# Moving a norm beside the other half's projection, finishing output projections tile by tile, and writing the output in four parts

## What is computed

```python
x = x + gt1 * y_lat
x = x + gt2 * squared_relu_mlp(modulate_2(rms_norm(x, norm2_g[i]), sh2, sc2), mlp_w1[i], mlp_w2[i])
if not last:
    ctx = ctx + mods_c[2] * y_ctx
    ctx = ctx + mods_c[5] * squared_relu_mlp(modulate_2(rms_norm(ctx, norm2_g[i]), mods_c[3], mods_c[4]), mlp_w1[i], mlp_w2[i])
```

## Time and profile before

| what | value |
|---|---|
| median of 3 runs | 3119.28 us |
| lowest and highest run | 3113.44 and 3119.92 us |
| profiled execution, first to last instruction (span) | 3114.3 us |
| own time of the profiled execution | not listed apart from the three runs |
| mean granted clock of TensorE | 0.967 of full |
| TensorE busy | 2933.0 us |
| VectorE, ScalarE busy | 1225.4, 714.7 us |
| moved by DMA | 687.00 MB, 221 GB/s |

### The profile page before, as it was taken

How to read it: one execution, slowest core, us unless ns; L and a number is a source line. 1 busy time by engine, 2 the same in 40 slices (tenths; PEclk the granted TensorE clock), 3 DMA queues, 4 the chain that set the end, 5 groups by cost and what they waited for, 6 DMA issues and landing times.

```text
span 3114.3 us, 51962 instructions
## 1 busy us (share of the span) xinstructions
PE 2933.0 (94%) x23528; PEld 2024.0 (65%) x23528; DVE 1225.4 (39%) x2176; ACT 714.7 (23%) x1144; POOL 47.5 (2%) x37
## 2 busy tenths in 40 slices
PE   5898998998999999999999899889999999988898
PEld 5788997877333333333333466689999885687898
DVE  5668853242111101101101277445555443454454
ACT  2224333131000000000000112334333322311343
POOL 0000000000000000000000000000000000032000
PEclk8899999999999999999999999999999999999999
DMA  7756764536899999999999322046566431010452
GB/s 288 290 201 256 286 232 170 196 120 253 327 364 358 364 368 372 356 362 376 366 354 364 135 68 95 1 149 230 217 230 227 166 123 53 1 71 6 165 182 82
DMA packets 96947, 687.00 MB, mean 221 GB/s; under 512 B 10576, under 2 KB 13776, under 8 KB 13904
## 3 DMA queue, kind: packets, MB, share of 16 engines
q1 hardware_dynamic: 94064, 678.47, 56.6%
q10 hardware_dynamic: 2656, 5.14, 0.4%
HBM read 682.52 MB, written 1.05 MB: 219 GB/s over the span
## 4 chain that ended last, share of the span: by engine, by line
PE 90%; DVE 6%; ACT 3%; DMA 1%; issue 1%; POOL 0%; DVEq 0%; ACTq 0%
PE ps L485 40%; PE ps L1942 19%; PE ps L821 11%; PE ps L1965 7%; PE ps L732 6%; PE ps L1968 3%; PE ps L496 2%; PE ps L709 1%; PE ps L1950 1%; DMA XT<-XIN 1%; DVE macc L578 1%; ACT HT L670 1%; DVE FR L802 0%; DVE RN L680 0%; DVE AR L2438 0%
## 5 line engine op out<-in xcount | busy, mean ns | idle before, releaser
L1942 PE MATMUL ps<-AR 128*32 128x512 f32 x4080 | 533.5, 592 | 0.0
L485 PE MATMUL ps<-HT,ring 128*128 128x256 f32 (+1 forms) x1696 | 446.2, 424 | 9.6 <-ACT HT L670 9.6
L485 PEld LDWEIGHTS ps<-HT,ring 128*128 128x128 f32 x1696 | 326.6, 194 | 122.4 <-issue 79.7
L485 PE MATMUL ps<-FR,FR 128*128 128x256 f32 x3120 | 389.9, 285 | 1.7 <-DVE M_moe_mod L587 1.7
L485 PEld LDWEIGHTS ps<-FR,FR 128*128 128x128 f32 x3120 | 379.5, 192 | 11.5 <-issue 9.5
L2053 DVE TENSOR_TENSOR AR<-AR,ps 128x256 f32<-128x256 f32 x84 | 35.5, 423 | 802.1 <-ACT AR L2017 802.1
L821 PE MATMUL ps<-FR,FR 128*128 128x256 f32 x2832 | 349.3, 283 | 0.0
L821 PEld LDWEIGHTS ps<-FR,FR 128*128 128x128 f32 x2832 | 343.9, 192 | 0.8 <-issue 0.8
L1942 PEld LDWEIGHTS ps<-AR 128*32 128x32 f32 x4080 | 150.8, 110 | 297.0 <-issue 294.5
L802 DVE TENSOR_TENSOR FR<-ring,FR 128x2048 fp32r<-128x2048 f32 x129 | 294.4, 2291 | 116.1 <-ACT FR L786 116.1
L786 ACT ACTIVATE FR<-ring 128x2048 fp32r<-128x2048 f32 x129 | 244.6, 1906 | 120.2 <-PE ps L821 92.6
(11 more groups left out here) (411 smaller groups left out, 2603.6 us busy)
## 6 DMA issues: line engine op xcount, KB each, us to landing
ring<-W SPq DMA_DIRECT2D x441, 1024.0 KB, 6.2
AR<-W SPq DMA_DIRECT2D x205, 1024.0 KB, 7.9
XT<-XIN ACTq DMA_DIRECT2D x2, 1024.0 KB, 16.8
cst<-CS ACTq DMA_DIRECT2D x1, 1851.0 KB, 35.7
out<-XT SPq DMA_DIRECT2D x1, 1024.0 KB, 4.5
sml<-SM ACTq DMA_DIRECT2D x1, 986.5 KB, 32.5
cst<-CS ACTq DMA_DIRECT2D x1, 129.5 KB, 7.6
C<-SM ACTq DMA_DIRECT2D x1, 4.0 KB, 5.2
```

Source lines behind the costliest of these rows:

```text
L485: ins = g.matmul(out, l, r, **kw)
L1942: ins = g.matmul(bank.ap[group(i), :], mo.hg[e % 2][:, 4 * h + k, group(t)], w[n][:, k, :], start=j == 0 and k == 0, stop=j == 1 and k == ...
```

## The change

1. `early_step` replaces the rule of the background steps in block 0's network: one step in each of the 17 rounds of half 0 and in the first six of half 1. The rest of `ada1` no longer stands in the odd mixer.
2. `down_slot` and `down3` go through their last slot tile by tile (`down_order`), both k of a tile before the next, and raise an event `two` after every second tile; `residual_dve` waits for these one after another.
3. In `even_pe` the norm's sums of m0, half 0, come after the first slot of `ev.down1`. `ev.end` is gone. VectorE does the residual of half 0, the first low half, the norm of half 0, two more low halves, and then the residual of half 1. ScalarE makes three high halves before round 0. The banks of `ev.down1` are kept until round 1. The buffers ev.C and ev.oD, which the projection reads, are put at the end of the arena, behind the network's splits.
4. In m0's second half the norm of the odd mixer's half 0 is made: squares on ScalarE after round 8, sums on TensorE after round 9, root after round 10, products and shift after round 11. The banks of `m0.down1` are kept until the second input projection.
5. The output is written in four transfers of two tiles each, each issued once the second of its tiles is done.

```diff
+def early_step(block, c, r):
+    return 1 if block == 0 and (c == 0 or r < 6) else 0
...
+        def down_order(last):
+            return [(kk, m) for m in range(8) for kk in range(2)] if last else [(kk, m) for kk in range(2) for m in range(8)]
...
-            for kk in range(2):
-                k = 2 * i + kk
-                for m in range(8):
+            for kk, m in down_order(i == n - 1):
...
+                if i == n - 1 and kk == 1 and m in (1, 3, 5):
+                    ins.then_inc(*s.done("two", x, m // 2))
...
         def residual_dve(g, s, x, ready, M, gate_at, c=0):
-            s.wait_ge(*ready)
             for m in range(8):
+                s.wait_ge(*(("two", x, m // 2) if m < 6 else ready))
...
             for i in range(4):
                 out(1, i, [("ev.og", 3)] if i == 2 else [])
-            down_end("ev.down1")
-            s.mark("ev.end")
+                if i == 0:
+                    norm_pe(g, s, "m0")
...
-            for c in range(2):
-                residual_dve(g, s, f"ev.down{c}", ("down", f"ev.down{c}", 3), MN["ada0"][0], 16, c)
-            s.mark("ev.end")
+            residual_dve(g, s, "ev.down0", ("down", "ev.down0", 3), MN["ada0"][0], 16, 0)
...
         def mlp_pe(g, s, q, bg):
-            norm_pe(g, s, p)
-            s.wait_marks(mlp_before(q)[1], "TVAG")
+            if q:
+                norm_pe(g, s, p)
+                s.wait_marks("od.end", "TVAG")
...
+                    if n == 1 and q == 0:
+                        down_end("ev.down1")
...
-                    if q == 0 and (r % 2 or r % 4 == 2):
-                        bg.go()
+                    bg.go(early_step(q, c, r))
...
+                    if n == 16 + 9:
+                        norm_pe(g, s, "odd")
...
         def mlp_act(g, s, q):
...
             shift_act(g, s, p, MN[f"ada{q}"][0], 24, mlp_pairs(q)[0])
+            if q == 0:
+                w.make_act(g, s, 3)
...
+                    if n == 16 + 8:
+                        squares_act(g, s, "odd", odd_ready(s), 0)
+                    if n == 16 + 10:
+                        norm_root_act(g, s, "odd", 0)
+                    if n == 16 + 11:
+                        shift_act(g, s, "odd", MN["ada1"][0], 0)
...
         def mlp_dve(g, s, q, bg):
...
+            if q == 0:
+                w.make_dve(g, s, 3)
+                residual_dve(g, s, "ev.down1", ("down", "ev.down1", 3), MN["ada0"][0], 16, 1)
...
-                    if q == 0 and (r % 2 or r % 4 == 2):
-                        bg.go()
+                    bg.go(early_step(q, c, r))
+                    if n == 16 + 11:
+                        norm_dve(g, s, "odd", HT, mod_weight("ada1", 0))
...
-            norm_pe(g, s, "odd", (0,))
             b = counts.take("od.f1")
             s.wait_emptied(b)
             mm(g, b.ap[0:64, 0:256], [(sm("hy_w1", p=(0, 33)), cs("zT", p=(0, 33)))]).then_inc(*s.done("od.f1_ps"))
-            bg.finish("ada1")
-            s.wait_marks("m0.end")
             norm_done(s, "odd", (0,))
             both("od.in", 0)
             norm_pe(g, s, "odd", (1,))
             both("od.in", 1)
+            down_end("m0.down1")
...
+            for k in (0, 2, 4, 6):
+                s.wait_ge("norm.x", "fin1", k + 1, 0)
+                g.dma_start(OUT.rearrange("(k p) t -> p k t", p=128)[:, k:k + 2, :], XT[:, k:k + 2, 0:256]).then_inc(s_out, 16)
             s.barrier("end")
-            g.dma_start(OUT.rearrange("(k p) t -> p k t", p=128), XT[:, :, 0:256]).then_inc(s_out, 16)
-            g.wait_ge(s_out, 16)
+            g.wait_ge(s_out, 64)
```

More of the change, by code:

```diff
@@ L725, in down_slot @@
                 s.wait_ge(*one_ready)
[L726 to L733 removed]
+            for kk, m in down_order(i == n - 1):
+                k, h = 2 * i + kk, m % 2
+                if k == 0:
+                    s.wait_emptied(acc[m // 2])
+                ins = g.matmul(acc[m // 2].ap[:, h * 256:h * 256 + 256], w[:, kk, m * 128:m * 128 + 128], rhs(k),
+                               start=k == 0 and h == 0, stop=k == 2 * n - 1 and h == 1, skip_group_check=True)
+                if i == n - 1 and kk == 1 and m in (1, 3, 5):
+                    ins.then_inc(*s.done("two", x, m // 2))
             ins.then_inc(*s.done("down", x, i, frees=(sl,) if free else ()))
@@ L811, in up3, with down3 @@
             return mm(g, out, [q for k in range(8) for q in three([x[:, k, :] for x in v], [x[:, k, :] for x in hs])])
[L813 to L823, removed]
+        def down3(g, s, x, pair, i, n, acc, hid):
+            w = [v.rearrange("p (k c) -> p k c", k=2) for v in pair]
+            for kk, m in down_order(i == n - 1):
+                h = m % 2
+                if i == 0 and kk == 0:
+                    s.wait_emptied(acc[m // 2])
+                for j, (l, r) in enumerate(three([v[:, kk, m * 128:m * 128 + 128] for v in w], [v[:, kk, :] for v in hid])):
+                    ins = g.matmul(acc[m // 2].ap[:, h * 256:h * 256 + 256], l, r,
+                                   start=i == 0 and kk == 0 and h == 0 and j == 0,
+                                   stop=i == n - 1 and kk == 1 and h == 1 and j == 2, skip_group_check=True)
+                if i == n - 1 and kk == 1 and m in (1, 3, 5):
+                    ins.then_inc(*s.done("two", x, m // 2))
             return ins
@@ L1399, in dense_pe @@
                     s.wait_ge("dn.lo", i).wait_ge("dn.d_lo", n - 1)
-                    down3(g, s, w.pair(i), n - 1, 11, acc, [x[:, (n - 1) % 3, :, :] for x in de.d]).then_inc(*s.done("dn.used", i))
+                    down3(g, s, "dn.down", w.pair(i), n - 1, 11, acc, [x[:, (n - 1) % 3, :, :] for x in de.d]).then_inc(*s.done("dn.used", i))
                 bg.go()
@@ L2522, in mlp_pe @@
                         s.wait_ge(p + ".lo", i).wait_ge(p + ".d_lo", n - 1)
-                        down3(g, s, w.pair(i), r - 1, 16, acc, [x[:, (n - 1) % 3, :, :] for x in m.d]).then_inc(*s.done(p + ".used", i))
-                    if q == 0 and (r % 2 or r % 4 == 2):
-                        bg.go()
-                    if n == 4 and T == 512:
+                        down3(g, s, f"{p}.down{c}", w.pair(i), r - 1, 16, acc, [x[:, (n - 1) % 3, :, :] for x in m.d]).then_inc(*s.done(p + ".used", i))
+                    bg.go(early_step(q, c, r))
+                    if n == 4 and q == 0:
                         norm_pe(g, s, p, (1,))
-                for k in range(4):
-                    counts.drop(f"{p}.down{c}", k)
+                    if n == 16 + 9:
+                        norm_pe(g, s, "odd")
+                if q or c == 0:
+                    down_end(f"{p}.down{c}")
             s.mark(p + ".end")
@@ L2533, in mlp_act @@
             m, p, T = ml[q], f"m{q}", 512 - 256 * q
-            ready, before = mlp_before(q)
-            norm_act(g, s, p, ready(s))
-            s.wait_marks(before, "TVAG")
+            norm_act(g, s, p, mlp_ready(s, q))
+            if q:
+                s.wait_marks("od.end", "TVAG")
             w = Splits(p, m.names, m.fr, PARTS, from_ring)
```

33 lines of the change are left out of this document (15 added, 18 removed).

## The result

| | before | after |
|---|---|---|
| median, four runs of each | 3117.38 us | 3091.45 us |
| lowest and highest run | 3113.44 and 3119.92 | 3088.98 and 3093.42 |
| span of the profiled execution | 3114.3 | 3089.8 |
| mean granted clock of TensorE | 0.967 | 0.970 |

The ratio is 0.992, interval 0.9909 to 0.9932: 25.9 us less by the medians, 24.5 by the spans. Forecast were 3093.6 us and a gain of 25.7. The gain agrees to 0.2 us and the time to 2.2: the forecast started from 3119.28, the median of three runs of the kernel before, and over four runs it is 3117.38. The profiled execution itself took 3091.74 us, 1.9 more than its span. Most lines of the file moved down: the earlier trace rows speak of L709 and L691, which are L713 and L695 now, L821 is L828, L485 is L489.

What follows compares the result with a forecast made beforehand. TensorE, busy 94%, bounds the kernel, its idle time at a few seams deciding. 11.06 + 8.8 - 0.4 + 3.9 + 2.3 = 25.7 us off the median 3119.28 gives 3093.6 us, range 3082 to 3107.

Steps and rivals of the forecast that it cites:

- Part 1: Even mixer to m0: norm of m0's latent half beside the context projection removes idle time and slow clock; gain 11.06 us.
- a seam keeps its wait: Rival: norm done early, but m0's first up-projection waits for another thing; 11.06 us back, 3104.7 us; chance 0.14.
- Part 2: m0 to odd mixer: norm of the odd mixer's latent half inside m0's second half; gain 8.8 us.
- Part 3: Background steps move forward; neutral on TensorE except a longer wait between m0's halves; loss 0.4 us.
- rival of the starved rounds: Slower rival: m0's rounds with three slots each let the weight ring fall behind; 3128.1 us at 1.5 us a round; chance 0.05.
- Part 4: Last slot tile by tile wins only idle time before norm sums at ssm, odd and m1: 1.3 us each, 3.9 together.
- whole-residual rival: Each of three norm sums at ssm, odd and m1 gets its 3.23 us; 5.8 us more gone, 3087.8 us; chance 0.06.
- Part 5: Program's end: output in four parts, the last landing 2.2 us after its issue; gain 2.3 us.
- rival of outputs in a row: Output parts go one after the other at the program's end; 2.3 becomes -2.0 us, 3097.9 us; chance 0.06.
- slow 8.59 us: m0's first up-projection group, 5.92 us one group later; two causes left undivided: waiting for low halves, and clock at 0.50.

Runs made afterwards that it cites:

- run with 7 us of cover: Changed kernel with the norm's sums of m0 moved behind the third slot of the context projection instead of the first; 3096.3 us, ratio 0.9942.
- run without cover: Changed kernel with the norm's sums of m0 moved behind the fourth and last slot of the context projection; 3106.13 us, ratio 0.9963.
- the last one: Changed kernel with m1's first split made early, eight output transfers, and two background steps moved behind the residuals they stood before; 3081.79 us, ratio 0.9888.
- plain-order: Changed kernel, run twice, with each last slot through all eight tiles for one k, then the other, residual after the last matmul; 3100.47 and 3097.77 us.
- keep-busy run: Changed kernel with 17 matmuls whose result nobody reads behind m1's norm sums, to keep TensorE busy; 3094.91 us, ratio 0.993.
- unedited kernel: The changed kernel run once more without any edit, beside later experiments; 3088.94 us, ratio 0.9909.

## Why the prediction was right

*Part 1.* The two timelines decided it: TensorE waits for low halves that VectorE had been free to make for 25 us. Cost and mechanism held, with 11.4 for 11.06 and 9.9 when undone. The condition for full gain was a chain of 13.5 us and a queue of about 18 under a cover of 20.9. From the end of the sums, 2039.20, the chain took 12.8 us, to 2052.02, and the queue with its two low halves 18.6, to 2057.77. (The prediction speaks of ten steps of VectorE in the chain; there are sixteen, a product and a low half for each of eight k, and they took 6.4 us for its 7.) The run with 7 us of cover shows the loss on the other side of that condition, and the rival "a seam keeps its wait" is what the run without cover looks like: 11.0 us lost in the trace for its 11.06. (Its median of 3106.13 is near the rival's 3104.7 by chance, as it has some us of other stages in it.)

*Part 2.* 8.8 to 9.0 for 8.8; undone, 7.7. The difference is mostly how far the clock fell behind the idle time, 9.24 us for the projection there and 10.14 in the earlier trace rows.

*Part 3.* The wait between the halves went from 0.97 to 1.33. The cost was 0.36 for 0.4, and the rounds stayed free: TensorE was busy in 203.00 of 203 us of the first half's rounds and in 100.00 of 100 us of the second's, so the rival of the starved rounds falls. No experiment undoes this part; in the last one the wait goes with the step's place, as this account says.

*Part 4.* 1.2 to 1.3 at each of three places, and none at dense. The whole-residual rival falls: the sums still take 3.6 us. What the two plain-order kernels lost beyond it, 7.7 and 3.2 us in the scan, no step foresaw.

*Part 5.* Landing after 2.2 us as reckoned from the earlier trace rows: 1.47 fixed and 0.76 of data. The Trainium skill, "DMA: Bandwidth & Descriptors", section "Anatomy of one DMA", with some 2.0 us fixed, would have 2.6 by estimate; the trace has 2.2, so here the measurement decides. The section's fit is for transfers issued on GpSimd's path, which the prediction did not say, and these go out on SyncE's queue. The rival of outputs in a row falls, since the four issues begin within 2.4 us of each other and the last lands with its own 2.2.

*The one reading to correct.* The prediction left open how the slow 8.59 us in the earlier trace rows divides, and counted all of it at m0 as gain. That is right at m0, where both causes went. But before m1 the keep-busy run shows that the clock alone is worth nothing: 8.22 us pass from the first group to the second at either clock, because VectorE hands over that late. At m0 the kernel before has 8.43 us between the same two starts, so by estimate (8.43 - 8.22) only 0.2 us of it were the clock's, and nearly all of the 2.7 was waiting for VectorE.

## What to carry to other kernels

Where an in-order engine waits for a chain of small steps on two others, look at when the chain's *input* was ready, not at the chain: here it was ready 25 us earlier, and the two early norms made 20 of the 26 us. The cover has to hold the chain and what is queued behind it on the helping engines; with 7 us for a chain of 13 over a third of the gain was lost (4.1 of 11.0). Before speeding up a slow group, ask whether its successor waits for somebody else: the time from start to start tells, not the group's own duration.

## What was not expected

The granted clock costs by where it falls, and it falls in different places in runs of the same kernel. The state-space stage from norm to norm took 297.5 us in one trace of the changed kernel and 294.5 in another. Late in the scan it fell in both plain-order traces and in no other, for 17 and 7 us. In the 15 us ahead TensorE had been busy 4.0 to 4.2 of every 5 us, as it was in the unedited kernel, whose clock stayed up. The idle time of a fixed chain, on the other hand, repeats to 0.01 us (8.22 before m1 in every kernel that left it alone), and so do most stages behind the even mixer to 0.1, so there a stage read from traces tells 1 us where medians of four to six runs, which reach over 3 to 16 us, do not.
